# A projection's last column chunk, tile by tile: an encoder step on one Trainium2 core

## What is computed

```
x = x + concat(A, B, C) @ W_out[l]          # mixer: band attention, retention, convolution
x = x + CrossAttn(RMSNorm(x), memory)       # 4 heads over 256 memory tokens, ends in  o @ wx_o[l]
x = x + FFN(RMSNorm(x))                     # dense in layer 0, top-2 of 8 experts in layer 1
```

## Time and profile before

| | us |
|---|---|
| median of 3 runs | 1915.87 |
| lowest and highest run | 1913.7 and 1917.25 |
| the profiled execution's own time | 1910.14 |
| its span, first to last instruction | 1908.3 |
| tensor engine busy in it | 1728.4 |
| mean granted clock of the tensor engine | 0.966 |

### The profile page before, as it was taken

The page is one execution under the profiler, slowest core; times in us unless marked ns, Lnnn a source line. Parts: engine busy times, 40 slices in busy tenths (PEclk is TensorE's granted clock), DMA queues, the critical chain, the costliest instruction groups (busy, mean ns, idle before and its releaser), DMA issues.

```text
span 1908.3 us, 20073 instructions
## 1 busy us (share of the span) xinstructions
PE 1728.4 (91%) x7598; PEld 1205.1 (63%) x7598; DVE 788.9 (41%) x1140; ACT 605.9 (32%) x802; POOL 124.1 (7%) x243
## 2 busy tenths in 40 slices
PE   6998799878998998999969988889999999999996
PEld 3454546646787778644545575676776667666764
DVE  1621424233333232334133323364564457544753
ACT  1104113333222222110321232243554345434541
POOL 2230200000000000303011000000000000000000
PEclk9999899998999999999989999969999999999998
DMA  7525333272423332432533407258887888778783
GB/s 234 181 90 170 111 124 132 77 284 97 149 94 125 112 110 77 141 116 88 184 120 113 154 23 266 96 212 287 279 294 250 275 290 293 251 267 298 274 271 124
DMA packets 174553, 340.28 MB, mean 178 GB/s; under 512 B 6890, under 2 KB 48124, under 8 KB 174224
## 3 DMA queue, kind: packets, MB, share of 16 engines
q1 hardware_dynamic: 162224, 316.17, 49.0%
q0 software_dynamic: 3920, 12.58, 2.2%
q10 hardware_dynamic: 8352, 10.75, 1.6%
HBM read 329.43 MB, written 11.90 MB: 179 GB/s over the span
## 4 chain that ended last, share of the span: by engine, by line
PE 85%; ACT 6%; DVE 5%; issue 2%; DMA 1%; POOL 0%; ACTq 0%; SPq 0%; DVEq 0%; POOLq 0%
PE bank L910 20%; PE bank L949 13%; PE bank L951 12%; PE bank L950 12%; PE bank L1031 10%; PE bank L897 4%; PE bank L1050 3%; PE bank L927 2%; PE bank L1380 2%; ACT arena L1446 2%; DVE arena_parts L701 2%; ACT arena_parts L697 2%; PE bank L1078 1%; DMA ring<-in_w_in 1%; PE bank L1334 1%
## 5 line engine op out<-in xcount | busy, mean ns | idle before, releaser
L949 PE MATMUL bank<-arena_parts,features_parts 128*128 128x512 f32 (+1 forms) x960 | 375.1, 391 | 33.5 <-DVE arena_parts L701 21.6
L950 PE MATMUL bank<-arena_parts,features_parts 128*128 128x512 f32 (+1 forms) x960 | 369.2, 385 | 0.0
L701 DVE TENSOR_TENSOR arena_parts<-ring,arena_parts 128x2048 fp32r<-128x2048 f32 (+1 forms) x116 | 247.2, 2142 | 122.4 <-ACT arena_parts L697 122.4
L910 PE MATMUL bank<-ring,features_T 128*128 128x512 f32 (+1 forms) x672 | 271.0, 565 | 2.8 <-ACT features_T L1446 2.8
L697 ACT ACTIVATE arena_parts<-ring 128x2048 fp32r<-128x2048 f32 (+1 forms) x116 | 206.7, 1795 | 114.9 <-PE bank L951 114.1
L951 PE MATMUL bank<-arena_parts 128*128 128x512 f32 (+1 forms) x612 | 239.2, 391 | 0.0
L949 PEld LDWEIGHTS bank<-arena_parts,features_parts 128*128 128x128 f32 x960 | 184.1, 192 | 71.1 <-issue 16.4
L910 PEld LDWEIGHTS bank<-ring,features_T 128*128 128x128 f32 x672 | 127.7, 191 | 142.2 <-issue 136.0
L950 PEld LDWEIGHTS bank<-arena_parts,features_parts 128*128 128x128 f32 x960 | 184.2, 192 | 30.8
L1446 ACT ACTIVATE arena<-bank 128x512 f32<-128x512 f32 (+3 forms) x160 | 86.2, 566 | 347.8 <-PE bank L910 202.8
L951 PE MATMUL bank<-arena_parts,features_parts 128*128 128x512 f32 (+1 forms) x480 | 181.6, 378 | 0.0
(11 more groups left out here) (272 smaller groups left out, 1831.7 us busy)
## 6 DMA issues: line engine op xcount, KB each, us to landing
ring<-in_moe_w_up SPq DMA_DIRECT2D x40, 1024.0 KB, 5.2
ring<-in_moe_w_down SPq DMA_DIRECT2D x30, 1024.0 KB, 5.7
ring<-in_w_in SPq DMA_DIRECT2D x20, 1024.0 KB, 5.5
ring<-in_moe_w_gate SPq DMA_DIRECT2D x20, 1024.0 KB, 5.2
mem_kv<-in_moe_w_gate SPq DMA_DIRECT2D x20, 1024.0 KB, 5.3
ring<-in_cache_mem_k SPq DMA_DIRECT2D x16, 1024.0 KB, 7.0
ring<-in_cache_mem_v SPq DMA_DIRECT2D x16, 1024.0 KB, 7.0
ring<-in_moe_w_gate SPq DMA_DIRECT2D x20, 768.0 KB, 4.6
```

Source lines behind the costliest of these rows:

```text
L701: nc.vector.tensor_tensor(self.part(s, 1), self.raw(s), self.part(s, 0).bitcast(F32), ALU.subtract).then_inc(self.split, 1)
L910: ins = nc.tensor.matmul(out[:, 0:w], left(k, t), wt[:, k - k0, :], start=(g == 0 and k == k0), stop=(g == len(groups) - 1 and k == k0 + n ...
L949: nc.tensor.matmul(out, left[0], right[0], start=start, stop=False)
L950: nc.tensor.matmul(out, left[0], right[1], start=False, stop=False)
```

## The change

The last column chunk (c = 1) of "out" and of "o" is worked off tile by tile: for each token tile all eight row blocks in a row, with both half slabs at hand from the start. Chunk 0 stays as it was. In `slabs()` the first half slab of chunk 1 of "out" is now freed when tile 2 of the chunk is done, and not tile 0. The programs of VectorE, ScalarE and GpSimd are the same.

```diff
@@ slabs(), product @@
-                last = tiles - 1 if half or (c == 0 and key[0] == "in") else 0
+                last = tiles - 1 if half or (key[0], c) in (("in", 0), ("out", 1)) else 0
@@ the tensor engine's program @@
+            def last_chunk(key, name, left, c):
+
+                wt = [slab(name).rearrange("p (k n) -> p k n", k=4) for _ in range(2)]
+                for t in range(NT):
+                    b = begin(*key, c, t)
+                    for k in range(KC):
+                        ins = nc.tensor.matmul(b[:, :], left(k, t), wt[k // 4][:, k % 4, :],
+                                               start=(k == 0), stop=(k == KC - 1))
+                    end(ins, *key, c, t)
...
-                for c in range(2):
-                    product(("out", l), "w_out", oT_at, halves, 512, NT, c)
+                product(("out", l), "w_out", oT_at, halves, 512, NT, 0)
+                last_chunk(("out", l), "w_out", oT_at, 1)
...
-                for c in range(2):
-                    split_product(("o", l), l, 4 + 2 * c, oT_parts, c)
+                split_product(("o", l), l, 4, oT_parts, 0)
+                wt = [w_parts(l, m) for m in (6, 7)]
+                for t in range(NT):
+                    b = begin("o", l, 1, t)
+                    for g in range(2):
+                        ins = split_tile(b, oT_parts, 4 * g, wt[g], t)
+                    end(ins, "o", l, 1, t)
```

## The result

The changed kernel takes 1930.77 us in the median of 4 runs (1930.67 to 1933.47); the kernel before, run beside it on the same chip, takes 1914.78 (1912.15 to 1917.25). The ratio is 1.0087, 95% interval 1.007 to 1.0105: slower by 16.0 us. The forecast was 1924.0 with a range of 1919 to 1928, so the side was right and the size too small. The profiled execution of the changed kernel took 1930.80 us, 0.03 from its median; that of before, 1910.14 us, lies 4.6 us under the median of the 4 runs here. So the two traces differ by 20.7 us, of which the medians show 16.0. Executions of one and the same kernel scatter here by some 20 us, so the medians of many rounds decide, and single traces only show where a time sits.

What follows compares the result with a forecast made beforehand. The tensor engine was taken as the bound, with 85% of the span. 0 behind "out", 6.4 for two stalls and 1.9 for the clock made +8.3 us on the 1915.87 us median: 1924 us, range 1919 to 1928.

Steps and rivals of the forecast that it cites:

- Out: Mixer's output projection, both layers: tile 0 finishes earlier, but the 1.84 us idles behind it stay; 0 us saved or added.
- The slab freed later: Third query slab, issued later at 307.4 us, still lands 1.7 us before ScalarE takes it; 0 us, far end 3.0.
- The stall: Last chunk of "o": tensor engine waits for VectorE's subtraction of slab 7, 3.19 us late per layer; 6.4 us together.
- What the early tiles give back: Behind "o": tiles 0 and 1 finish earlier, but the tensor engine's waits there stay; 0 us.
- The clock: Behind the two stalls in "o": lower clock at three-in-five odds, 1.6 us each; 1.9 us, ends 0 and 3.4.
- The early tiles pay: Rival, chance 0.06: tiles 0 and 1 pace normalisation behind the projections, so 8.7 us of waits go; 1915.5 us.
- faster: Rival, chance 0.03: the same pacing also removes the 6.41 us wait at the dense stage's start; 1909.0 us.
- The order costs nothing: Rival, chance 0.05: VectorE reaches slab 7's subtraction in "o" before it is needed, so nothing changes; 1915.9 us.

Runs made afterwards that it cites:

- e1: The changed kernel with the cross attention's projection "o" put back, so only "out" goes tile by tile; 1914.74 against 1915.91 us for the kernel before, 0.9997.
- e3: The kernel before, old order of products, but the last chunk of "o" waits for both half slabs at its start; 1931.63 against 1915.91 us, 1.0091.
- e4: The changed kernel, with VectorE subtracting slab 7 right behind slab 6, two adds earlier; 1913.41 against 1915.91 us for the kernel before, 0.9986.
- e8: The changed kernel with slab 7 subtracted early and tile 1's row normalised right behind its add; 1919.93 against 1914.22 us before, ratio 1.0000.
- e2: The changed kernel with "out" and its line in slabs() put back, so only "o" goes tile by tile; 1930.38 us, 1.0078 of the kernel before.
- e5: The kernel before, with the wait for both half slabs ahead of the last "o" chunk in layer 0 alone; 1927.47 against 1914.22 us, 1.0054.
- e6: The kernel before, with the wait for both half slabs ahead of the last "o" chunk in layer 1 alone; 1920.05 against 1914.22 us, 1.0018.
- e9: The kernel before, with 7 throwaway matmuls and no wait ahead of the last "o" chunk of layer 0; 1922.76 against 1913.59 us, 1.0039.
- e7: The changed kernel with 13 throwaway matmuls in each wait for slab 7; 1921.45 against 1914.22 us for the kernel before, 1.0029.

## Why the prediction was right on the side and wrong on the size

**"Out": 0, right.** Tile 0's add moved to 295.52 (forecast 295.6), the transposes still start without a wait, and the engine still idles 1.85 us for the remainder that follows them, in the changed kernel's timeline:

```profile
295.52 0.68 DVE L1895 TENSOR_TENSOR x<-bank,x 128x512 f32<-128x512 f32 x1
...
306.76 1.04 PE L897 MATMUL bank<-consts,arena 128*128 128x128 f32 x8
...
308.09 1.29 DVE L1871 TENSOR_TENSOR arena_parts<-bank,features_parts 128x512 fp32r<-128x512 f32 x2 [0.45 <-ACT features_parts L1473]
...
309.64 0.47 PE L959 MATMUL bank<-arena_parts,features_parts 128*128 128x512 f32 x1 [1.85 <-DVE arena_parts L1871]
```

e1 puts the whole part at 0.9997.

**The slab freed later: 0, right.** The query slabs landed 6.1 us after issue in the median instead of 5.1, still early enough: ScalarE takes the third one at the same moment as before, with no wait. The transfers' row and ScalarE's row in the changed kernel:

```profile
ring<-in_wx_q SPq DMA_DIRECT2D x4, 1024.0 KB, 6.1
```

```profile
314.10 1.92 ACT L800 ACTIVATE arena_parts<-ring 128x2048 fp32r<-128x2048 f32 x1
```

**The stall: 6.4, right.** Idle 3.03 us and delay 3.19 us in layer 0, exactly as worked out; 6.1 us of new waiting in all. That it is the cause, e3 shows (the wait alone: 15.7 us) and e4 (the same order without it: no change).

**What the early tiles give back: 0, right.** All the waits behind the two projections stayed. e8 shows why freeing tile 1's row does not help either: tile 2's row is next in line, and it is last in either order.

**The clock: 1.9, wrong; this is the step that failed.** The prediction charged the lower clock at the two stalls only, at odds of three in five, and put it at nothing for everything behind them. By the medians the rest behind the stalls is 16.0 - 6.4 = 9.6 us, five times the term. Two things were mis-sized:

- "Three in five of 1.6 us at two places" took the lottery of the dense idles over to the stalls. After the change both stalls were followed by the lower clock, and so were those in the traces of e2, e3, e5 and e6: eight of eight, at 0.54 to 0.57. By the prediction's own reckoning that took 4.0 x 0.43 + 3.7 x 0.46 = 3.4 us in the changed kernel, in place of 1.9. The Trainium skill (TensorE: Matmul & The Clock Gate, section "Why this matters for your kernels") warns that an idle gap between bursts sends the engine back to half clock; the stalls of these traces agree with it, and the two unpunished idles of five in rows 9 do not. Its price for this was worked out as 3.2 us instead of 1.9, so the rule alone would have mended 1.3 us of the 7.7 that were missing.
- The greater part lies where no wait was added. The prediction paid for the clock only next to the stall. But in the changed kernel's trace the dense stage pays at idles where it went free before, +5.30 us, and layer 1 behind it +3.52. e5 and e6 share out the whole roughly (together they make 19.1 by the medians and 13.8 by the ratios): 13.3 for the stall in layer 0, which has these stages behind it, and 5.8 for the one in layer 1, behind which the experts stage is unchanged (+0.05). e9 shows that it can come without any idle in "o".

The prediction had the evidence in its hand: its own rows 9 show equal idles with unequal outcomes. It read that as a chance of three in five at the new stall. It should also have asked what happens to the old idles behind the stall: two of the five had gone free in that one trace, and another execution could pay for them. That the change makes this likelier is what the runs show and no row of before could.

**The rivals.** "The early tiles pay" and "faster" fell by e4 and e8. "The order costs nothing" is wrong for the change as it stands, because VectorE does take the add first; e4 makes it true by an earlier subtraction.

**What stays open.** What decides whether an old idle is followed by the lower clock. Not the idle's length (the same idle has both outcomes), nor the moment in the program (22 against 30 throwaway matmuls, and e1 against before). A kernel without the stall is not always spared: beside e1's trace, the profiled execution of e4, one of its two longest at 1928.57 us, spent 322.18 us in the dense stage and 412.36 in layer 1, as this view of its stages shows:

```profile
484.01:806.19 322.18, 298.92 (x1334) 0.95 0.33 111
806.19:1218.55 412.36, 369.23 (x1609) 0.95 0.41 137
```

The stall does not make a cost that the kernel never had; it turns one that most executions are spared (10 of e4's 12 lie at or under 1916.54 us) into one that nearly all pay. A spared run with both stalls would lie at or under 1916.54 + 6.4 + 3.4 = 1926.3 us, an estimate from the figures above. Of the 16 runs of e2, e3 and the changed kernel only one does, e3's of 1925.97, and its trace has the dense stage at 319.86 us but layer 1 at 406.37, so it paid in the first alone. Why a stall makes the extra so much likelier is not shown. Why the totals of 15 and 30 throwaway matmuls lie 2.6 and 4.7 us above their work stays open too. A version clearly faster than the kernel before was not found; e4 (0.9986, 0.9962 to 1.001) comes nearest and is no change.

## What to carry to other kernels

Before a loop is turned so that one output tile takes all its row blocks at once, ask when its last operand is ready: the old order hid slab 7's subtraction behind 36 matmuls of slab 6, and the new one needs it at the start. If it is late, move its producer forward first (here an earlier subtraction in VectorE's program took 16 us back to nothing that can be measured). And when a stall in a chain of matmuls is priced, add to its length the clock behind it, and count the idles further down that so far went free as a risk: here 6 us of waiting cost 16. Take more than one execution before calling such an idle free.

## What the runs showed of the hardware that was not expected

- The length of an idle of the tensor engine does not fix its price: the same 1.25 us idle of the dense stage is followed by 3.4 us at 0.50 in the changed kernel and by 1.00 before.
- The clock of a stage can change with no change in its code. The dense stage had 0.98 and 314.62 us in the trace of before, 0.96 and 319.84 us behind 7 throwaway matmuls without an idle, and 0.95 and 322.06 us in e1's trace, where it was entered as before.
- Filling a wait with useless matmuls, without shortening it, took back 9 to 10 of 16 us (e7: 1.0029, 1.0001 to 1.0056, against 1.0087).
- Executions of one kernel without the stall differ by as much as the change costs: of e1's 12 runs, 9 lie between 1910.3 and 1915.2 us at mean granted clocks of 0.962 to 0.966, and 3 between 1922.0 and 1927.2 at 0.956 to 0.958.
